# Four buffers for the modulation rows, and a unit summed over partitions by one-column matmuls, in a two-layer decoder trunk

## The reference

```python
cond = jax.nn.silu(c)                                      # (1, 1024)
for l in range(2):
    if l == 1:                                             # second layer: shared keys and values
        kv_mod = (cond @ w_kv_ada + b_kv_ada).reshape(b, 2, d)
        kv = modulate(x, kv_mod[:, 0], kv_mod[:, 1]) @ w_kv_b
    mod = (cond @ w_ada[l] + b_ada[l]).reshape(b, 9, d)
    h = modulate(x, mod[:, 0], mod[:, 1])                  # x * (1 + scale) + shift
    x = post_norm_residual(x, swiglu(h, w_ffn_in[l, 0], w_ffn_out[l, 0]), mod[:, 2], 0.5, ...)
    ...                                                    # attention with mod[:, 3:6]
    ...                                                    # second FFN with mod[:, 6:9]
```

## Time and profile before

| | us |
|---|---|
| median of 3 runs | 1076.11 |
| lowest, highest | 1076.07, 1076.93 |
| the profiled execution | 1077.93 |
| its span, first to last instruction | 1076.1 |
| PE busy | 1021.9 |
| DVE busy | 776.7 |
| ACT busy | 522.4 |

### The profile page before, as it was taken

How to read it: one execution, slowest core, us unless ns; L and a number is a source line. 1 busy time by engine, 2 the same in 40 slices (tenths; PEclk the granted TensorE clock), 3 DMA queues, 4 the chain that set the end, 5 groups by cost and what they waited for, 6 DMA issues and landing times.

```text
span 1076.1 us, 12357 instructions
## 1 busy us (share of the span) xinstructions
PE 1021.9 (95%) x4708; PEld 827.7 (77%) x4708; DVE 776.7 (72%) x908; ACT 522.4 (49%) x852; POOL 85.7 (8%) x160
## 2 busy tenths in 40 slices
PE   3799999999999899999999999999999899999997
PEld 1587888877787677888878888888877777888885
DVE  7578777688775798777777587777877768445485
ACT  1545444446555734444466544444466755434342
POOL 0011111001000011111100011111100000000010
PEclk9899999999999999999999999999999999999999
DMA  9979898955774299889847399888946447555551
GB/s 360 353 260 332 298 322 277 355 198 163 268 250 142 78 316 339 302 300 321 310 184 234 122 309 337 309 296 318 328 164 218 150 147 252 177 196 167 187 194 39
DMA packets 147490, 265.61 MB, mean 247 GB/s; under 512 B 8424, under 2 KB 98920, under 8 KB 147432
## 3 DMA queue, kind: packets, MB, share of 16 engines
q1 hardware_dynamic: 124448, 182.87, 49.5%
q0 software_dynamic: 20928, 75.53, 19.9%
q10 hardware_dynamic: 2056, 6.42, 1.9%
HBM read 263.75 MB, written 1.05 MB: 246 GB/s over the span
## 4 chain that ended last, share of the span: by engine, by line
PE 66%; DVE 16%; DMA 7%; ACT 6%; issue 4%; DVEq 0%; SPq 0%; ACTq 0%
PE psum L1253 13%; PE psum L1255 13%; PE psum L1254 13%; PE psum L1328 7%; PE psum L1330 7%; PE psum L1329 7%; DMA ada<-in_w_ada 6%; DVE w_lo L837 5%; DVE acc L869 5%; ACT w_hi L504 2%; PE psum L1361 1%; PE psum L1288 1%; ACT psum L593 1%; PE psum L1275 1%; DVE qT L980 1%
## 5 line engine op out<-in xcount | busy, mean ns | idle before, releaser
L837 DVE TENSOR_TENSOR w_lo<-raw,w_hi 128x2048 fp32r<-128x2048 f32 x164 | 371.3, 2286 | 59.1 <-ACT w_hi L504 59.1
L1253 PE MATMUL psum<-w_hi,hT_hi 128*128 128x512 f32 x896 | 357.9, 399 | 8.4 <-DVE w_lo L837 8.1
L1255 PE MATMUL psum<-w_hi,hT_lo 128*128 128x512 f32 x896 | 351.0, 392 | 0.0
L1254 PE MATMUL psum<-w_lo,hT_hi 128*128 128x512 f32 x896 | 350.0, 391 | 0.0
L504 ACT ACTIVATE w_hi<-raw 128x2048 fp32r<-128x2048 f32 x164 | 310.4, 1915 | 0.4 <-PE psum L1330 0.4
L1253 PEld LDWEIGHTS psum<-w_hi,hT_hi 128*128 128x128 f32 x896 | 168.9, 189 | 46.2 <-DVE w_lo L837 7.7
L508 ACT ACTIVATE tmp<-psum 128x256 f32<-128x256 f32 x88 | 33.8, 384 | 348.0 <-PE psum L1255 348.0
L869 DVE SCALAR_TENSOR_TENSOR acc<-ada,cond,acc 128x1024 f32<-128x1024 f32 x128 | 164.1, 1282 | 51.8 <-DMA ada<-in_w_ada 41.5
L1255 PEld LDWEIGHTS psum<-w_hi,hT_lo 128*128 128x128 f32 x896 | 168.9, 188 | 36.5
L1254 PEld LDWEIGHTS psum<-w_lo,hT_hi 128*128 128x128 f32 x896 | 169.3, 189 | 33.0
L1328 PE MATMUL psum<-w_hi,a_hi 128*128 128x512 f32 x368 | 150.5, 409 | 0.8 <-ACT kT L666 0.8
(11 more groups left out here) (151 smaller groups left out, 727.5 us busy)
## 6 DMA issues: line engine op xcount, KB each, us to landing
raw<-in_w_ffn_in SPq DMA_DIRECT2D x176, 512.0 KB, 5.0
ada<-in_w_ada POOLq DMA_DIRECT2D x128, 512.0 KB, 5.4
raw<-in_w_ffn_out SPq DMA_DIRECT2D x88, 512.0 KB, 6.0
raw<-in_w_qkv_a SPq DMA_DIRECT2D x24, 512.0 KB, 5.1
raw<-in_w_o SPq DMA_DIRECT2D x16, 512.0 KB, 4.3
ada<-in_w_kv_ada POOLq DMA_DIRECT2D x16, 512.0 KB, 5.2
raw<-in_w_kv_b SPq DMA_DIRECT2D x16, 512.0 KB, 6.4
raw<-in_w_ada SPq DMA_DIRECT2D x4, 1024.0 KB, 14.2
```

The source lines that it names most:

```text
L837: nc.vector.tensor_tensor(lo_of(n), slot_of(n), hi_of(n).bitcast(F32), ALU.subtract)\
L1253: nc.tensor.matmul(dst, s_hi, m_hi, start=start, stop=False)
L1254: nc.tensor.matmul(dst, s_hi, m_lo, start=False, stop=False)
L1255: return nc.tensor.matmul(dst, s_lo, m_hi, start=False, stop=stop)
```

## The change

**Rows.** A unit's rows take four places in the FFNs: the two of `ada` and the two halves of `z`. A table `ROW_AT` gives each row its place, the count of loads of that place, and the accumulation after which the place is free. The gates made during projections (units 7 and 18) keep two places, because `z` holds queries then. Where `z` was last used by a norm, row 2 of the unit also waits for `x_scaled` (`FREED_BY`, three units).

**Sums.** `sum_unit` takes the place of `turn_unit` for the twelve units in the FFNs: eight f32 matmuls with a block of `acc` as weights and one column of -1 as the moving operand. Each gives 128 sums in one PSUM column; ACT reads the eight columns at once with a factor of -1. The sum needs no room of the turned tiles, and stands earlier in the step: after the second `wide`, before `turn_inner`, behind the wait for `inner_lo` of the step before. ACT's `keep_unit` moves ahead of `inner_hi`. The two first units are turned as before (under new names).

```diff
+def row_places():
+    loads, last, found = [0] * 4, [0] * 4, {}
+    for u in range(STAGED // 4, UNITS):
+        for row in range(8):
+            p = row % (2 if u in PROJECTION_GATES else 4)
+            loads[p] += 1
+            found[u, row] = (p, loads[p], last[p])
+            last[p] = 8 * u + row + 1
+    return found
+
+PROJECTION_GATES = [GATE_OF[1], GATE_OF[4]]
+ROW_AT = row_places()
+FREED_BY = {unit(KV, 0): 1, unit(1, 3): 2, unit(1, 8): 4}
...
+        ada_rows = [ada[:, 0, :], ada[:, 1, :], z[:, 0, :], z[:, 1, :]]
+        unit_sums = misc[1][:, 256:256 + KT]
...
                 for row in range(8):
-                    pool.wait_ge(acc_steps, 8 * u + row - 1)
-                    pool.dma_start(ada[:, row % 2, :], ada_view(w)[:, row, j * D:(j + 1) * D])\
-                        .then_inc(ada_in[row % 2], 16)
+                    place, _, free = ROW_AT[u, row]
+                    if free:
+                        pool.wait_ge(acc_steps, free)
+                    else:
+                        pool.wait_ge(acc_steps, 2 * STAGED)
+                    if row == 2 and u in FREED_BY:
+                        pool.wait_ge(x_scaled_done, 2 * FREED_BY[u] + 2)
+                    pool.dma_start(ada_rows[place], ada_view(w)[:, row, j * D:(j + 1) * D])\
+                        .then_inc(ada_in[place], 16)
...
                     silu(f, s, 1)
+                    if first_unit is not None and s % 2 == 0:
+                        keep_unit(first_unit + s // 2 - 1)
                     inner_hi(f, s, 0)
                     split_hi(n + 3 * s + 4)
-                    if first_unit is not None and s % 2 == 0:
-                        keep_unit(first_unit + s // 2 - 1)
...
+            def keep_unit(u):
+                act.wait_ge(unit_out, u + 1)
+                nc.scalar.activation(modT[:, u, :], unit_sums, ACT.Copy, scale=-1.0).then_inc(mod_ready, 1)
...
+                        place, loads, _ = ROW_AT[u, 2 * q + r]
+                        part = ada_rows[place]
+                        dve.wait_ge(ada_in[place], 16 * loads)
...
+            def sum_unit(u):
+                pe.wait_ge(acc_steps, 8 * u + 8)
+                for k in range(KT):
+                    last = nc.tensor.matmul(unit_sums[:, k:k + 1], acc[:, k * P:(k + 1) * P], neg_ones[:, 0:1],
+                                            start=True, stop=True)
+                last.then_inc(unit_out, 1)
...
                     wide(pairs[s], 1)
                     inner_done(f, s - 1, 0)
+                    if first_unit is not None and s % 2 == 0:
+                        inner_done(f, s - 1, 1)
+                        sum_unit(first_unit + s // 2 - 1)
                     turn_inner(f, s, 0)
...
                     inner_done(f, s - 1, 1)
-                    if first_unit is not None and s % 2 == 0:
-                        inner_done(f, s, 0)
-                        turn_unit(first_unit + s // 2 - 1)
                     add_rows(o, inner(s - 1), 1, first=s == 1).then_inc(w_used, 1)
```

More of the change, by code:

```diff
@@ L253, in build @@
         w_used = sem("w_used")
-        ada_in = [sem(f"ada_in{i}") for i in range(2)]
+        ada_in = [sem(f"ada_in{i}") for i in range(4)]
         staged_in = [sem(f"staged_in{i}") for i in range(STAGED + 1)]
@@ L546, in ffn, with keep_first_half @@
                 nc.scalar.preload_act_table(ACT.Sqrt)
-            def keep_unit(u, tiles=KT):
+            def keep_unit(u):
+                act.wait_ge(unit_out, u + 1)
+                nc.scalar.activation(modT[:, u, :], unit_sums, ACT.Copy, scale=-1.0).then_inc(mod_ready, 1)
+            def keep_first_half(u, tiles):
                 act.wait_ge(unit_out, u + 1)
@@ L640, in _ @@
             nc.scalar.activation(rowsT[:, :], misc[1][:, 0:256], ACT.Copy).then_inc(rows_ready, 1)
-            keep_unit(0, KT // 2)
-            keep_unit(1, KT // 2)
+            keep_first_half(0, KT // 2)
+            keep_first_half(1, KT // 2)
             for t in range(TT):
@@ L847, in accumulate @@
                         sums = acc0
[L848 to L852, removed]
+                elif q == 0:
+                    dve.wait_ge(unit_out, u)
                 for r in range(2):
-                    if u >= STAGED // 4:
-                        dve.wait_ge(ada_in[r], 64 * (u - STAGED // 4) + 16 * q + 16)
+                    if u < STAGED // 4:
+                        part = src[:, r, :]
+                    else:
+                        place, loads, _ = ROW_AT[u, 2 * q + r]
+                        part = ada_rows[place]
+                        dve.wait_ge(ada_in[place], 16 * loads)
                     if 4 * u + q == STAGED - 1 and r == 1:
@@ L860, in accumulate @@
                         if u not in GATE_OF:
-                            nc.vector.tensor_scalar(sums, src[:, r, :], factor, None, ALU.mult).then_inc(acc_steps, 1)
+                            nc.vector.tensor_scalar(sums, part, factor, None, ALU.mult).then_inc(acc_steps, 1)
                             continue
@@ L868, in accumulate @@
                         base = sums
-                    nc.vector.scalar_tensor_tensor(out=sums, in0=src[:, r, :], scalar=factor, in1=base,
+                    nc.vector.scalar_tensor_tensor(out=sums, in0=part, scalar=factor, in1=base,
                                                    op0=ALU.mult, op1=ALU.add).then_inc(acc_steps, 1)
@@ L1282, in turn_x, with turn_first_unit @@
                 last.then_inc(turned, 2)
-            def turn_unit(u, sums=acc):
+            def sum_unit(u):
[4 more added lines that the diff above has]
+                last.then_inc(unit_out, 1)
+            def turn_first_unit(u, sums):
                 pe.wait_ge(acc_steps, 8 * u + 8)
@@ L1470, in _ @@
             pe.wait_ge(rows_ready, 1)
-            turn_unit(0, acc0)
+            turn_first_unit(0, acc0)
             stay_busy(START_PRODUCTS[0])
@@ L1475, in _ @@
             pe.wait_ge(second_half_kept, 1)
-            turn_unit(1)
+            turn_first_unit(1, acc)
             pe.wait_ge(x_in, 16 * TT)
```

## The result

Timed beside the kernel before, six runs each, the changed kernel takes **1081.34 us** (1079.46 to 1082.37) against 1076.15 (1075.80 to 1076.94): a ratio of 1.0044, 95% interval 1.0031 to 1.0057, or +4.7 us with 3.3 to 6.1 (the ratio is of the means; the two medians lie 5.2 apart). It is slower by less than half a per cent, and the forecast was 1083.1 with its own range from 1080.5. The profiled execution took 1081.94 us with a span of 1080.1, so the two profiled spans differ by 4.0.

What follows compares the result with a forecast made beforehand. PE was taken to bound the kernel; +10.6 us for the sums and -3.6 for the holes gave +7.0 on the median 1076.11, so 1083.1 us. Its own range was 1080.5 to 1086 (chance 0.60), the wider one 1078 to 1091.

Steps and rivals of the forecast that it cites:

- What bounds the kernel: PE, busy 1021.9 of 1076.1 us: work added to or taken off it moves the span unless it fills a hole.
- The pass with one column: In each summed unit on PE: 16 passes at 0.11 us, 1.76 us, 0.88 more than before; +10.6 us for twelve units.
- Rivals A and C: Sum's passes on PE: A, load hides, 0.06 us each, 1073.5 us, chance 0.12; C, nothing overlaps, 0.19, 1098.4, chance 0.08.
- The holes: PE's idle gaps behind late rows in the first two FFNs go with four buffers: -3.6 us, between 0 and -3.6.
- The three named holes: Step 2 of the first FFN, 1.16 us; the same in the second, 0.97; the end of the first, 1.50.
- no other hole of PE follows a row: Claim that only the three counted holes of PE come from late rows, so the gain is at most 3.6 us.
- no row of a unit decides: Claim on PE's other holes, at the start, at w_lo after the norms and in the attention stages: no unit's row causes them.
- Rival B: Holes move to the sum's new place, PE waiting 1.2 and 1.0 us there: +10.6 alone, 1086.7 us, chance 0.12.
- The new place: Sum right after the step's second wide product, 3 us earlier; a_lo in time once row waits go, remaining delay absorbed: 0.
- At no price: ACT's earlier read, DVE and POOL's new wait for x_scaled: 0; the start: 0, up to 4 us at the upper end.
- rival D: PE's clock falls during the twelve sums, where hardly a column streams: +19.7 us more, 1102.8 us, chance 0.04.
- Rival E: No effect beyond the three holes and a small price: whole kernel within 0.2%, chance 0.04.

Runs made afterwards that it cites:

- experiments 3 and 4: On the changed kernel: one product instead of eight, 1064.13 us; 32 columns, 1079.77; sixteen bf16 passes on zeros, 1066.69; one-pass fp32r sums, minus_r declared last, 1070.99.
- experiment 1: Four row buffers with the eight transposes of the kernel before, 1072.08 us; the changed kernel's sums at their new place with two row buffers, 1082.42 us.

## Why the prediction was right

**What bounds the kernel.** Work put on PE shows up in the span: one block instead of eight moved the profiled span by 18.2 us where the rows of PE had 18.7.

**The pass with one column.** This was the step with the least under it, a delay of 0.05 us in one kind of place, and it held: 0.11 for each of sixteen. Rivals A and C fall with the 1.70 us in each of the twelve units. Part of this is luck. The 0.05 was read as a load with too little to hide behind, but the earlier trace rows has a delay of 0.08 in the product behind the transposes as well, whose loads had 0.11 each; a slow start behind a short product would explain both, and the 0.05 alone could not tell it from a load. That the streaming does not take the 0.11 was argued; experiments 3 and 4 show it (32 columns, bf16, one pass instead of two). The unit comes out 0.85 dearer, not 0.88: 1.74 with what the turn adds, where 1.76 was set, and 0.89 saved, where the 0.90 read in the earlier trace rows had been rounded to 0.88. That is +10.2 against +10.6.

**The holes.** Here a term was mis-sized: -5.4, not -3.6. The three named holes were right to a tenth of a microsecond (1.2, 1.0, 1.5). What failed is the sentence "no other hole of PE follows a row". Five more follow one, of 0.2 to 0.4 us, at the ends of the FFNs, where DVE had waited for a row one or two steps ahead and was still late with a_full. The row at 227.97 above shows why they are easily missed: it starts 0.35 us late, but its recorded idle time is 0.17, because the record before it ends 0.17 after the next product could have started, and its releaser is DVE's tmp, with no transfer in sight. Still, PE's own list of waits in the kernel before had three of the five:

```profile
PE psum L1361 <- DVE tmp L894: 2.9, 5, 1.3
```

Of these five places the prediction used one, the 1.3. One more, 1.1 us at 386.19, follows no row and is there in the changed kernel too; the other three are 0.17 each and went with the rows. The last two of the small holes have recorded idle times of 0.02 and 0.04 and are in no list. The sentence that "no row of a unit decides" in the attention stages failed as well: the 3.44 us at 842.50 follow one. That did not touch the sum, since the change leaves that hole as it is.

**Who takes the holes away.** The prediction gave them to the buffers, and set a price on the waits for rows without asking which of them were waits for PE. By the traces of experiment 1 either part alone is nearly enough. Rival B, in which they stay, falls: PE has no wait at the sum, and none before the turn near 221 us.

**The new place.** Costed at nothing, and PE has no wait at the sum, as foreseen. The late place would cost 1.2 us more, by the slow start of a second product, which the prediction did not see.

**At no price.** ACT, DVE and POOL: no new wait of PE's came from them. The start: -0.3 in this pair of executions, inside what it varies by. The clock (rival D): the granted clock is 1.00 around the unit. In the second layer's attention stage it falls to 1.2 GHz for a part of two stretches, one of them behind PE's 3.58 us of waiting shown above, where the kernel before has one such stretch. It costs next to nothing there: PE is 3.8 us behind the kernel before ahead of that stage and 4.0 behind it at the end. Rival E falls too, since the interval of the ratio starts at 1.0031. Windows of the changed kernel (us, busy by engine, clock, DMA share, GB/s):

```profile
84.00:88.00 4.00, 4.00 (x29) 3.64 (x28) 2.41 (x2) 0.90 (x4) 0.28 (x1) 1.00 0.89 340
...
834.00:840.00 6.00, 6.00 (x36) 5.46 (x35) 4.50 (x9) 4.11 (x9) 1.05 (x2) 0.77 1.02 318
...
846.00:850.00 4.00, 4.00 (x17) 3.59 (x18) 3.30 (x9) 3.08 (x4) 0.00 (x0) 0.63 0.00 0
```

**The sum.** +10.2 - 5.4 - 0.8 is 4.0 between the two profiles, and 4.7 by the timed runs. Predicted were 7.0: against the profiles 1.8 were missed on the holes, 0.4 on the units and 0.8 on small differences, all to the same side. The measured 1081.34 lies 0.8 us above the lower end of the stated range, so a little more of the same would have left it.

## What to carry to other kernels

Here a matmul with one column was priced by its stationary operand. Count the 128x128 loads and whether the type makes it one load or two, and compare with what a transpose costs, which here was one load for the same block. When two edits come together, time each alone: here one of them gained 3 us and the other lost 8, and the gain could be had by itself. When the holes behind a cause are counted, go from each wait of that cause forward to the bounding engine, in every stage. Before a slower time is put down to an edit, see whether the instructions that it does not touch kept their length: a tile declared in the middle moves all behind it.

## What the runs showed of the hardware

- Start to start, a pass of one or of 32 columns takes 0.11 us (1.70 for sixteen) with an f32 stationary operand of 128x128, in two passes for each product; with fp32r 0.10 to 0.11 (0.80 for eight) and one pass for each product; with bf16 0.026 (0.41 for sixteen).
- The wide products (512 columns, fp32r) follow each other at 0.2274 us or at 0.233, by where the tiles lie in relation to each other: 8 or 64 bytes put between acc and x_sb made the kernel 2% slower (1100.76 and 1101.22 us), 64 bytes ahead of all tiles did not (1081.35). The loss is the same while DVE, ACT and POOL stand idle and no transfer is in flight (0.2269 against 0.2333 and 0.2334). The granted clock (0.99) and every instruction were the same, and each was timed beside the kernel before, at 1075.14 us for the first two and 1075.98 for the last.
- The first wide product behind a short one is about 0.1 us late in letting its successor start, whatever the short one was: 0.31 behind eight transposes, 0.32 behind the turn, 0.33 behind the sum.
